# Other rounds for the late projection halves, the gate sigmoids, the weight roundings and the taps of an attention stage

## The reference

```python
h = rmsnorm(x, norm1_g)
q, k, v, glu_a, glu_b, g_attn, g_conv = split(h @ w_in + b_in)      # 512,512,512,512,512,1024,1024 columns
a = stick_breaking_attention(rmsnorm(q), rmsnorm(k), v) @ w_attn_out  # 8 heads of 64, causal
u = glu_a * sigmoid(glu_b)
c = silu(layernorm(depthwise_conv31(u))) @ w_conv_out + b_conv_out
x = x + (sigmoid(g_attn) * a + sigmoid(g_conv) * c) @ w_out
x = x + conv_ffn(rmsnorm(x))                                          # 1024 -> 5632 -> 1024
return rmsnorm(x)

def stick_breaking_attention(q, k, v):
    z = q @ k.T / 8                       # key s before query t only
    weights = sigmoid(z[t, s]) * prod(1 - sigmoid(z[t, j]) for s < j < t)
    return weights @ v
```

## Time and profile before

| | before |
|---|---|
| median of three runs | 1704.54 us |
| the profiled execution | 1699.73 us |
| its span, first to last instruction | 1697.8 us |
| mean granted TensorE clock | 0.996 |
| PE busy | 1647.2 us, 97% |
| DVE busy | 1131.3 us, 67% |
| ACT busy | 609.3 us, 36% |
| second block on PE | about 60 to 546 us |

### The profile page before, as it was taken

One profiled execution on the slowest core, in us unless ns is written; L12 is line 12 of the kernel. 1 busy time (PEld: TensorE's weight loads), 2 busy tenths in 40 slices (PEclk: granted clock), 3 DMA queues, 4 the chain that ended last, 5 costly groups with the idle time before them and its releaser, 6 DMA issues. The chain is left out here.

```text
span 1697.8 us, 26678 instructions
## 1 busy us (share of the span) xinstructions
PE 1647.2 (97%) x9802; PEld 1524.0 (90%) x9802; DVE 1131.3 (67%) x1628; ACT 609.3 (36%) x1541; POOL 102.7 (6%) x71
## 2 busy tenths in 40 slices
PE   7999999998999999999999999999999999999998
PEld 6997887887987999999989998999989999998996
DVE  5479799799796233444477665676656666665677
ACT  5446446446444234211154131322313122131224
POOL 0000000000000114332320000000000000000000
PEclk9999999999999999999999999999999999999999
DMA  5330320402313422723312020211102111020102
GB/s 187 84 79 20 93 58 20 126 26 58 92 69 122 157 78 93 242 87 90 102 38 87 26 63 13 62 44 43 49 25 62 33 42 61 25 62 17 57 13 108
DMA packets 145879, 119.42 MB, mean 70 GB/s; under 512 B 6763, under 2 KB 130127, under 8 KB 145800
## 3 DMA queue, kind: packets, MB, share of 16 engines
q1 hardware_dynamic: 145800, 118.35, 22.6%
HBM read 95.83 MB, written 22.50 MB: 70 GB/s over the span
## 5 line engine op out<-in xcount | busy, mean ns | idle before, releaser
L1638 PE MATMUL bank<-h2hi,whi 128*128 128x364 f32 (+1 forms) x1056 | 347.7, 329 | 2.1 <-PEq L1644 2.1
L1638 PE MATMUL bank<-h2lo,whi 128*128 128x364 f32 (+1 forms) x1056 | 347.6, 329 | 0.0
L1638 PE MATMUL bank<-h2hi,wlo 128*128 128x364 f32 (+1 forms) x1056 | 347.5, 329 | 0.0
L1423 DVE TENSOR_TENSOR x<-bank,x 128x512 f32<-128x512 f32 x270 | 181.1, 689 | 166.6 <-PE bank L1413 161.7
L1638 PEld LDWEIGHTS bank<-h2hi,whi 128*128 128x128 f32 x1056 | 199.0, 188 | 2.7 <-issue 2.3
L1638 PEld LDWEIGHTS bank<-h2lo,whi 128*128 128x128 f32 x1056 | 199.0, 188 | 0.4
L1638 PEld LDWEIGHTS bank<-h2hi,wlo 128*128 128x128 f32 x1056 | 199.0, 188 | 0.0
L815 DVE SCALAR_TENSOR_TENSOR c_sb<-u,dww,c_sb 128x1118 f32<-128x1118 f32 x120 | 165.8, 1382 | 2.7
L1413 PE MATMUL bank<-whi,mhi 128*128 128x512 f32 x342 | 133.7, 391 | 2.4 <-PEq L1433 1.2
L1413 PE MATMUL bank<-whi,mlo 128*128 128x512 f32 x342 | 133.3, 390 | 0.0
L1413 PE MATMUL bank<-wlo,mhi 128*128 128x512 f32 x342 | 133.3, 390 | 0.0
(11 more groups left out here) (206 smaller groups left out, 3398.5 us busy)
## 6 DMA issues: line engine op xcount, KB each, us to landing
wraw<-in_w_up SPq DMA_DIRECT2D x88, 256.0 KB, 3.2
wraw<-in_w_in SPq DMA_DIRECT2D x30, 512.0 KB, 5.0
wraw<-in_w_down SPq DMA_DIRECT2D x44, 256.0 KB, 2.8
scr_gate<-gst SPq DMA_DIRECT2D x11, 544.0 KB, 4.4
gch<-scr_gate SPq DMA_DIRECT2D x16, 364.0 KB, 3.7
xt<-in_x_prompt SPq DMA_DIRECT2D x8, 512.0 KB, 5.2
kpast<-in_cache_sb_k SPq DMA_DIRECT2D x16, 256.0 KB, 5.3
wraw<-in_w_out SPq DMA_DIRECT2D x16, 256.0 KB, 2.8
```

Of the source, the lines that this page charges most:

```text
L1423: dve.tensor_tensor(y, bank[banks[d % len(banks)]][:, :], y, ALU.add).then_inc(down_ev, 1)
L1638: mm = pe.matmul(bank[(3 * tau + c) % 4][:, 0:c1_ - c0], w[:, ws], x[:, k, c0:c1_], start=(k == 0 and n == 0), stop=(k == KT - 1 and n == 2))
```

## The change

The tables get other rounds; `GATE_ROUND` is gone, and window 3 follows the same table as the others. In rounds 12 to 14 (those with cached keys) the first half of the round goes ahead of the scores. In round 16 there are three late halves in place of four (in window 3 three in place of one), and the outputs of round 14 go ahead of the last transposes of q.

```diff
-AB_ROUND = {9: (0, 1), 10: (2,), 11: (3,), 12: (4,), 13: (5,), 14: (6,), 15: (7,), 16: (8, 9, 10, 11)}
-GATE_ROUND = {r: (2 * r, 2 * r + 1) if r < 13 else (13 + r,) for r in range(NR)}
-B_EVAC_ROUND, A_EVAC_ROUND = {10: 0, 14: 1}, {12: 0, 16: 1}
+LATE_ROUND = {9: (0,), 10: (1,), 11: (2,), 12: (3, 4), 13: (5, 6), 14: (7,), 15: (8,), 16: (9, 10, 11)}
+B_EVAC_ROUND, A_EVAC_ROUND = {11: 0, 14: 1}, {13: 0, 15: 1}
+GATE_EVAC_ROUND = {**{n + 1: n for n in range(9)}, 11: 9, 12: 10, 13: 11, 15: 12}
 NORM_ROUND = {11: 0, 12: 1, 13: 2}
-HI_ROUND, LO_ROUND = {9: 0, 10: 1, 13: 2}, {10: 0, 12: 1, 14: 2}
+HI_ROUND, LO_ROUND = {9: 0, 12: 1, 14: 2}, {10: 0, 13: 1, 15: 2}
...
 TAPS = dealt(
...
-             [[3, 2, 1, 1, 3, 2, 2, 2, 3, 2, 0, 0, 0, 0, 1, 3, 6],
-              [0, 3, 3, 1, 3, 3, 2, 2, 2, 2, 1, 0, 0, 0, 1, 3, 5],
-              [0, 3, 3, 2, 3, 2, 3, 2, 2, 2, 0, 0, 0, 0, 1, 3, 5],
-              [0, 3, 3, 3, 3, 3, 2, 2, 3, 1, 3, 3, 2, 0, 0, 0, 0]])
+             [[3, 2, 1, 1, 3, 2, 2, 2, 3, 0, 0, 0, 3, 0, 2, 2, 5],
+              [0, 0, 3, 3, 3, 3, 3, 2, 2, 1, 0, 0, 2, 1, 2, 2, 4],
+              [0, 0, 3, 3, 3, 3, 3, 3, 2, 0, 1, 0, 2, 1, 2, 1, 4],
+              [0, 0, 3, 3, 3, 3, 3, 3, 3, 1, 1, 1, 3, 3, 1, 0, 0]])
...
 # ScalarE, last window
-    if 1 <= r <= 13:
-        gate_evac(r - 1)
-    if r == 15:
-        gate_evac(13)
+    if r in GATE_EVAC_ROUND:
+        gate_evac(GATE_EVAC_ROUND[r])
...
+gate_evac(13)
 o_evac(3, 2)
...
 # TensorE
 def halves_of(p, r):
-    if p == PAIRS - 1:
-        return GATE_ROUND[r]
-    return (2 * r, 2 * r + 1) if r < NT else tuple(2 * NT + h for h in AB_ROUND[r])
+    return (2 * r, 2 * r + 1) if r < NT else tuple(2 * NT + h for h in LATE_ROUND[r])

 def window(p):
     for r in range(NR - 1):
         halves = halves_of(p, r)
+        if pasts_of(r):
+            half_(p, halves[0])
+            halves = halves[1:]
         if r < len(ROUNDS):
             scores(p, r)
...
-        half_(p, halves[-1])
+        for h in halves[-1:]:
+            half_(p, h)
...
     for x, h in enumerate(halves):          # round 16
-        if x == len(halves) - 1:
+        if x == 2:
             outputs(p, NR - 3)
+            if p < PAIRS - 1:
+                qk_transposes(p + 1, 4)
+                qk_transposes(p + 1, 5)
         half_(p, h)
-        if x < len(halves) - 1:
+        if x < 2 and p < PAIRS - 1:
             for n in (2 * x, 2 * x + 1):
                 qk_transposes(p + 1, n)
```

## The result

The change makes the kernel slower: 1708.32 us (median of 8, 1707.50 to 1711.48) against 1704.43 beside it (8 runs, 1701.05 to 1704.71), a ratio of 1.0031 [1.002, 1.0042], that is 3.4 to 7.2 us; the medians themselves differ by 3.9. The direction was forecast, the size was not: the forecast put 10.6 us on the median.

A forecast was written before the change was run, and what follows sets the result against it. PE was 97% busy, but DVE, nearly without idle time from round 2 to 11, was taken to set the pace there. Window terms 0.9 + 0.8 + 2.1 + 6.8 = +10.6 us on 1704.54 gave 1715.1, range 1709 to 1721.

The forecast's parts named there:

- The rule: Scores of round r+1 cannot start before the end of DVE's second scan of round r-1 plus 1.2 us.
- window 0: Attention block's window 0: -0.1 us from the moved halves and waits, plus a 1.0 wait for a_evac: +0.9.
- window 1: Attention block's window 1: DVE reaches round 9 some 1.7 us later, scores(11) +0.1; window end +0.8.
- window 2: Attention block's window 2: scores(11) 1.4 us later, cached keys' transposes unmoved; window end +2.1.
- window 3: Attention block's window 3: transposes 1.1 us later with three halves of 2.18 still to do; window end +6.8.
- Part 1: A half leads rounds 12 to 14: 1.8 us of waits a window go, -7.2, and window 3's 0.7 too.
- Part 2: Round 14 ends without a half: outputs wait 1.7 us for ACT's copy in each of four windows, +6.8.
- Part 3: Fewer halves in rounds 9 to 11: DVE's scans limit the gain, and halves return in rounds 12 to 16 at 2.18 us each.
- first bank wait: PE's first wait at the cached keys' transposes in windows 0 to 2, priced at 2.68 us each.
- The waits go and nothing else comes: Rival: ScalarE and VectorE run rounds 9 to 11 ahead of PE, halves only move; -6.8 us, 1697.7; chance 0.14.
- No change: Rival: DVE lags less in windows 1 and 2, whose 2.9 us aren't paid; +1.0, 1705.5; chance 0.12.
- The clock falls at the new waits: Rival: round 14's 1.7 us waits lower the clock, 1.7 each, 6.7 in four windows; 1721.8; chance 0.13.

The follow-up runs named there:

- before_fill: Kernel before plus 12 unused matmuls at the end of round 11 in windows 0 to 2; 1700.41 us, ratio 0.9985 [0.9975, 0.9995].
- after: The changed kernel's first profiled execution; 1707.56 us, attention block 464.64 us.
- after_a: The changed kernel, unchanged, profiled anew; 1707.35 us, attention block 465.03 us.

## Why the prediction was right in direction and wrong in size

**The rule: right. The window terms: near it, but for window 0.** On the scale of before (the windows start 0.88 and 0.66 earlier, 0.04 and 3.09 later), scores(11) came at 157.85, 274.97 and 392.75, forecast 157.83, 274.9 and 392.2; window 3's transposes at 514.19, forecast 513.9, its scores(11) at 507.5, beyond the 506 below which the forecast would have been wrong. The scan of round 10 ended 2.05 us later there (511.26 + 1.22 = 512.48), forecast 1.8.

| term | forecast | measured |
|---|---|---|
| window 0 | +0.9 | +0.2 |
| window 1 | +0.8 | +0.7 |
| window 2 | +2.1 | +3.05 |
| window 3 | +6.8 | +6.0 |
| sum, profiled execution against profiled execution | +10.6 | +9.9 |

**Part 1: right.** The waits for copied keys are gone and 0.7 with them. **Part 2: right,** the wait is 1.48 in each window, not 1.7. **Part 3: right** in place and cause; the wait for a_evac was 1.15, forecast 1.0, and the stage waits went to later rounds, as said, but cost 5.3 in place of 3.3. Window 0 was 0.7 too dear, though its two new waits came as forecast (1.15 and 1.48 for 1.0 and 1.7) and its transposes 0.3 later; what made that good isn't placed. Window 3's 6.8 was 0.8 too dear, though its transposes came 0.3 later than forecast: a half measured 2.07 (517.69 to 519.76) and not 2.18, three times, and round 14 gave 0.2; the rest I haven't placed.

**The step that failed** is the last one: "that execution is 4.8 below the median of the runs, and on 1704.54 the sum gives 1715.1". It takes the 4.8 as a constant that comes on top of both kernels. It isn't: the profiled execution of the kernel before lies 4.7 below the median of its eight runs, that of the changed kernel 0.8 below its own. The execution of before that was profiled is one in which the clock did not fall behind any of the three 2.68 us waits, and the change shortens just these waits. That "three waits of 2.68 left it at 1.00" was true of that execution, and the price of a first bank wait in windows 0 to 2 was put at 2.68 and no more. Profiled again, the same kernel had 1, 3 and 3 falls there. Its block is 457.5 on average over four executions (454.7 to 459.3), the changed one's 465.1 (464.6 to 465.6): 7.7 apart and not 9.9. The before_fill kernel shows it by time as well: with these waits filled it is 2.8 us faster. Its block, in the one execution profiled, is 1.2 longer than that of the kernel before without such falls (455.89, 454.71). So the falls are worth 2.8 us in the median run, or some 4.0 if the 1.2 are the filler's price; both are estimates. That leaves 9.9 - 4.0 = 5.9 to 9.9 - 2.8 = 7.1, against 3.9 and 5.5 timed by the medians and 5.3 by both ratios. The mis-sized term is thus the first bank wait: 2.68 us with, on the average, 0.9 to 1.3 more each (a third of 2.8 to 4.0).

The rest of the program, where both kernels are the same, took 1242.3 to 1245.4 us in these eight executions, on average 1.2 less after than before, and 2.1 less in the two executions that the sum was made for: so the changed kernel's profiled execution took 1707.56 and not the 1710.3 of the sum, with only 0.7 of that from the block. This second part of the miss stays open: it may be chance, and no run here settles it.

**The rivals.** *The waits go and nothing else comes* fell with the scores' 14.1 us; that DVE's total work is the same is true and beside the point, as in windows 1 to 3 it has no gap from round 2 to round 11 (in window 0 it has some of 0.5 to 0.7 us, before and after). *No change* (windows 1 and 2 unpaid) fell: they paid 3.75 in the profiled executions. *The clock falls at the new waits* was right about the chip and wrong about place and price. Round 14's waits, 1.48 us, had a full clock behind them in all four executions. The falls came behind the waits at line 221, where they cost nothing that shows, and behind the scores of rounds 10 and 11 (1.86 us in window 1 or 1.85 in window 2, and 2.65 to 2.81 in window 3). In window 3 these cost nothing that shows either: the sigmoids that PE needs next wait for DVE's scan, and PE reaches the transposes of cached keys 78.17 us into the window in after, with the clock down right before them, and 78.15 in after_a, with it full there. In window 1 it was 0.7 to 1.0 us (117.13 and 117.41 against 116.42), in window 2 1.2 to 1.6. The Trainium skill ("TensorE: Matmul & The Clock Gate", section "HAM oscillation — how this bites in real kernels") tells of a kernel whose bursts of matmuls are shorter than the waits between them, and which loses the clock at every one of these waits. This trace agrees in part only: the waits here are shorter than the work ahead of them (2.68 us behind the 4.97 from 158.59 to 163.56), and of twelve 2.68 us waits in the four executions of the kernel before seven had a fall behind them. The prediction took the one execution without such a fall for the rule.

## What to carry to other kernels

Where an engine looks 97% busy, find out which engine has no gap round by round, and don't take filler work out of the rounds in which that other engine paces: the same halves were free to PE there and took 2.07 us each where they came back. A sum made on one profiled execution holds at best for the part that it covers in that execution (here the block, 9.9 for 10.6); before it is carried to a median, profile the kernel again and see which waits have a fall of the clock behind them in some executions, above all where the change shortens one. Split a bundle of moves: here two that took load off the late engines, one of them from the bundle and one in another form, gave 11.6 us together, while the bundle, with its halves and its own taps, lost some 5.

## What the runs showed of the hardware

The clock behind a wait of the same length differs from execution to execution: 2.68 us had 1.00 behind it, or 0.50 to 0.72 over 6 us. Length alone doesn't order it within one execution either: 2.10 us (at 235.80) had 1.00 behind it, the same 2.10 at 352.86 had 0.72, and 1.86 (at 274.31) 0.72. A wait cut to 0.68 by extra matmuls had no fall in any of three windows, and with 12 matmuls more in each of them the kernel was 2.8 us faster. A fall cost 1.6 to 1.8 us in window 0 of the kernel before; behind the waits at line 221 and in window 3 of the changed kernel, where PE waits for DVE's chain next, no cost showed.
